# Gate matrix of an expert layer: indirect stores in place of one-hot products

## The reference

```
def peer_ffn(h, w_query, sub_keys, u_tab, v_tab):
    q = (h @ w_query).reshape(bsz, seq, 8, 2, 128)
    scores = einsum('blhcd,hckd->blhck', q, sub_keys)          # 8 heads, 2 halves, 128 keys
    s_top, i_top = top_k(scores, 16)
    cand_s = s_top[..., 0, :, None] + s_top[..., 1, None, :]   # 16 x 16 pairs
    cand_i = i_top[..., 0, :, None] * 128 + i_top[..., 1, None, :]
    best_s, pos = top_k(cand_s, 16)
    expert_idx = take_along_axis(cand_i, pos)
    gates = softmax(best_s)
    act = gelu(einsum('td,thkd->thk', h, u_tab[expert_idx]))
    return einsum('thk,thkd->td', gates * act, v_tab[expert_idx])
```

## Time and profile before

| what | value |
|---|---|
| median of 3 executions | 4148.32 us (4144.81 to 4148.98) |
| the profiled execution | 4145.28 us |
| its span, first to last instruction | 4143.5 us |
| stage one of the expert layer | about 2592 to 3417 us |
| stage two | 3419 us to the end |
| mean granted clock of TensorE | 0.946 of full speed |

### The profile page before, as it was taken

One profiled execution on the slowest core, in us unless ns is written; L12 is line 12 of the kernel. 1 busy time (PEld: TensorE's weight loads), 2 busy tenths in 40 slices (PEclk: granted clock), 3 DMA queues, 4 the chain that ended last, 5 costly groups with the idle time before them and its releaser, 6 DMA issues. The chain is left out here.

```text
span 4143.5 us, 48110 instructions
## 1 busy us (share of the span) xinstructions
PE 3751.7 (91%) x17280; PEld 3022.6 (73%) x17280; DVE 2600.6 (63%) x3745; ACT 1820.0 (44%) x1842; POOL 114.1 (3%) x171
## 2 busy tenths in 40 slices
PE   8779529999999999992999769999999999999999
PEld 4567427777777777771988547888888887888887
DVE  7326539999999999994442542887877534444444
ACT  1226217777777777771332422244444432222222
POOL 0000020000000000002000000000000000000000
PEclk9899759999999999995999779999999999999999
DMA  7410139999999999986322012344444446556554
GB/s 300 146 52 1 47 131 338 362 358 361 363 359 359 360 360 358 362 332 230 102 92 82 1 66 92 135 160 163 172 162 183 160 180 211 188 181 199 185 182 142
DMA packets 222108, 851.13 MB, mean 205 GB/s; under 512 B 19536, under 2 KB 89424, under 8 KB 146832
## 3 DMA queue, kind: packets, MB, share of 16 engines
q1 hardware_dynamic: 202800, 756.94, 51.1%
q10 hardware_dynamic: 9216, 58.72, 3.4%
q0 software_dynamic: 9952, 33.57, 2.4%
HBM read 745.91 MB, written 103.25 MB: 205 GB/s over the span
## 5 line engine op out<-in xcount | busy, mean ns | idle before, releaser
L1384 DVE TENSOR_TENSOR w_low<-w_raw,w_high 128x2048 fp32r<-128x2048 f32 x399 | 909.3, 2290 | 142.4 <-ACT w_high L1313 137.8
L1313 ACT ACTIVATE w_high<-w_raw 128x2048 fp32r<-128x2048 f32 x399 | 764.5, 1916 | 337.2 <-PE ps L125 190.3
L2335 DVE TENSOR_TENSOR uv_lo<-uv_raw,uv_hi 128x2048 fp32r<-128x2048 f32 x128 | 293.3, 2292 | 655.2 <-ACT uv_hi L2192 655.0
L123 PE MATMUL ps<-w_high,xT_high 128*128 128x512 f32 x1056 | 433.7, 411 | 21.1 <-issue 21.1
L124 PE MATMUL ps<-w_low,xT_high 128*128 128x512 f32 x1056 | 418.4, 396 | 0.0
L125 PE MATMUL ps<-w_high,xT_low 128*128 128x512 f32 x1056 | 417.9, 396 | 0.0
L123 PE MATMUL ps<-h4T_high,uv_hi 128*128 128x512 f32 x1024 | 410.4, 401 | 0.5 <-DVE uv_lo L2335 0.5
L123 PE MATMUL ps<-uv_hi,w_hi 128*128 128x512 f32 x1024 | 405.1, 396 | 2.6 <-issue 2.6
L125 PE MATMUL ps<-uv_hi,w_lo 128*128 128x512 f32 x1024 | 405.0, 396 | 0.0
L124 PE MATMUL ps<-uv_lo,w_hi 128*128 128x512 f32 x1024 | 405.0, 395 | 0.0
L125 PE MATMUL ps<-h4T_high,uv_lo 128*128 128x512 f32 x1024 | 399.4, 390 | 0.0
(11 more groups left out here) (481 smaller groups left out, 6281.7 us busy)
## 6 DMA issues: line engine op xcount, KB each, us to landing
w_raw<-in_w_gate_up SPq DMA_DIRECT2D x267, 1024.0 KB, 7.0
w_raw<-in_w_down SPq DMA_DIRECT2D x132, 1024.0 KB, 6.8
uv_raw<-in_peer_u SPq DMA_DIRECT2D x64, 1024.0 KB, 5.1
uv_raw<-in_peer_v SPq DMA_DIRECT2D x64, 1024.0 KB, 4.9
a_rows<-a_out SPq DMA_DIRECT2D x128, 256.0 KB, 2.1
g_rows<-spread ACTq DMA_DIRECT2D x16, 2048.0 KB, 6.5
qT<-g_rows SPq DMA_DIRECT2D x32, 1024.0 KB, 8.9
qT<-a_rows SPq DMA_DIRECT2D x64, 512.0 KB, 8.2
```

Source lines behind the costliest of these rows:

```text
L123: pe.matmul(out, l_hi, r_hi, start=first, stop=False)
L1313: act.activation(w_hi[:, n % SPLIT, :], w_raw[:, n % RAW, :], ACT.Copy).then_inc(s_wh, 1)
L1384: dve.tensor_tensor(w_lo[:, n % SPLIT, :], w_raw[:, n % RAW, :], w_hi[:, n % SPLIT, :].bitcast(F32), ALU.subtract).then_inc(s_wl, 1)
L2335: dve.tensor_tensor(uv_lo[:, n % 2, :], uv_raw[:, n % 2, :], uv_hi[:, n % 2, :].bitcast(F32), ALU.subtract).then_inc(s_lo, 1)
```

## The change

One-hots, gate products, their spreading and the turned selections are removed. In their place:

- A region of 32 MB in DRAM (`gates`) is filled with zeros by 32 stores of 1 MB on SP's queue, beside the first attention. GpSimd clears the source, 128 x 2048, ahead of it. SP waits for the zeros in the next block.
- VectorE works out for each picked expert of a token its place in that region. For each of the 8 heads it compares its 16 experts with all 128 of the token, adds up the gates of those that are equal and in the same or a later head, and sends a value whose expert already stood in an earlier head to a spare place behind the region.
- GpSimd stores the sums with indirect DMAs, 16 for each head, tile by tile: 4 x 8 x 16 = 512, each of 128 values of 4 bytes.
- A plan by estimated costs places VectorE's 45 steps of each tile, 8.2 us to a group.
- The first load of gates waits for all 512 stores, and reads whole rows of the new layout.

```diff
+    gates_flat = nc.dram_tensor("gates", [P * P * SEQ + SEQ * SEL, 1], F32, kind="Internal").ap()
+    gates = gates_flat[0:P * P * SEQ, :].rearrange("(p x) o -> p (x o)", p=P)
...
+    zeros = sb(stage, "zeros", [P, 4 * SEQ])
+    s_z0, s_gz = sem("zeros_here"), sem("gates_zeroed")
...
+            pool.memset(zeros[:, :], 0.0).then_inc(s_z0, 1)
...
+            sp.wait_ge(s_z0, 1)
+            for n in range(P // 4):
+                sp.dma_start(gates[:, n * 4 * SEQ:(n + 1) * 4 * SEQ], zeros[:, :]).then_inc(s_gz, 16)
...
+            sp.wait_ge(s_gz, 16 * (P // 4))
...
+    FIRST, SECOND, BEST, BEST_PLACES, BEST_SECOND, PASS = 4.0, 2.6, 3.4, 3.9, 3.7, 2.3
+    COSTS = [FIRST, SECOND] * 4 + [BEST, BEST_PLACES, BEST_SECOND] * 2 + [1.5 * PASS, PASS, PASS] * 2 + [1.0 * PASS]
+    COSTS += [x for h in range(PH) for x in (PASS, PASS + 0.9, PASS * (PH - h) / PH)]
+    UNIT_EXP, A_STEP = 14, 8.2
+    plan, scores_at, exp_at, spent, turn_of = [[] for _ in range(NG)], {}, {}, 0.0, [(i, x) for i in range(TT) for x in range(len(COSTS))]
+    for i, x in turn_of:
+        n = int(spent // A_STEP)
+        assert n < NG - 1
+        plan[n].append(i)
+        if x == 0 and i:
+            scores_at[n - 1] = i
+        if x == UNIT_EXP:
+            exp_at[n] = i
+        spent += COSTS[x]
...
             def load_weights(p):
                 if p == 0:
                     sp.wait_ge(s_scr, 4 * TT)
-                    sp.wait_ge(s_gst, 16 * (SEQ // HALF))
-                else:
-                    if p >= 2:
-                        sp.wait_ge(s_wf, 2 * (p - 1))
+                    for i in range(TT):
+                        sp.wait_ge(s_put[i], 16 * SEL)
+                elif p >= 2:
+                    sp.wait_ge(s_wf, 2 * (p - 1))
                 for m in (2 * p, 2 * p + 1):
                     sp.wait_ge(s_ast[m % NA], 16 * (m // NA + 1))
                 if p % 2 == 0:
                     q = p // 2
-                    sp.dma_start(g_in[:, q % 2, :].rearrange("p (h x) -> p h x", h=SEQ // HALF),
-                                 g_rows.rearrange("h p x -> p h x")[:, :, 2 * p * HALF:(2 * p + 4) * HALF])\
-                      .then_inc(s_gin[q % 2], 16)
+                    sp.dma_start(g_in[:, q % 2, :], gates[:, 2 * p * SEQ:(2 * p + 4) * SEQ]).then_inc(s_gin[q % 2], 16)
                 sp.dma_start(a_in[:, p % 2, :, :], a_rows.rearrange("m p n -> p m n")[:, 2 * p:2 * p + 2, :])\
                   .then_inc(s_ain[p % 2], 16)
 
...
+        @block.gpsimd
+        def _(pool):
+            pool.iota(token_f[:, :], [[P, TT]], base=0, channel_multiplier=1, allow_small_or_imprecise_dtypes=True).then_inc(s_tok, 1)
+            pool.iota(aside_f[:, :, :], [[P * SEL, TT], [1, SEL]], base=P * P * SEQ, channel_multiplier=SEL,
+                      allow_small_or_imprecise_dtypes=True).then_inc(s_tok, 1)
+            for i in range(TT):
+                for h in range(PH):
+                    pool.wait_ge(s_tot, i * PH + h + 1)
+                    for k in range(PT16):
+                        x = h * PT16 + k
+                        pool.indirect_dma_start(gates_flat, bass.IndirectOffsetOnAxis(ap=place[:, i % 2, x:x + 1], axis=0),
+                                                total[:, i % 2, h, k:k + 1], None).then_inc(s_put[i], 16)
...
-            def gate_products(r):
-                s = r % HOTS
-                pe.wait_ge(s_hot, 5 * (r + 1))
-                if r >= 2:
-                    pe.wait_ge(s_gt2, r - 1)
-                for q in range(4):
-                    mm = pe.matmul(ps[:, 6 + r % 2, q * P:(q + 1) * P], first_hot[:, s, q, :], second_hot[:, s, q, :],
-                                   start=True, stop=True)
-                mm.then_inc(s_gb, 1)
...
-                        if k % 2 and j * 4 + k // 2 in places[n]:
-                            gate_products(rounds.pop(0))
-                    if j == 0 and n in sel_at:
-                        turn_selected(sel_at[n])
...
-            def spread_round(r):
-                act.wait_ge(s_gb, r + 1)
-                h, at = divmod(r, RN)
-                if h and at == 0:
-                    act.wait_ge(s_gst, 16 * h)
-                act.activation(spread[:, :, 4 * at:4 * at + 4].rearrange("p k n -> p n k"),
-                               ps[:, 6 + r % 2, :].rearrange("p (n k) -> p n k", n=4), ACT.Copy).then_inc(s_gt2, 1)
-                if at == RN - 1:
-                    act.wait_ge(s_gt2, r + 1)
-                    act.dma_start(g_rows[h, :, :], spread_flat).then_inc(s_gst, 16)
...
+                first_k, second_k, gate_of = (sel[:, c, :, :].rearrange("p h k -> p (h k)") for c in range(3))
+                st(dve.scalar_tensor_tensor(out=second_k, in0=first_k, scalar=float(PK), in1=second_k, op0=ALU.mult, op1=ALU.add))
+                if i == 0:
+                    dve.wait_ge(s_tok, 2)
+                st(dve.scalar_tensor_tensor(out=place_f[:, :], in0=second_k, scalar=float(SEQ),
+                                            in1=token_f[:, i:i + 1].to_broadcast([P, SEL]), op0=ALU.mult, op1=ALU.add))
+                st(dve.tensor_tensor(to_aside[:, :], aside_f[:, i, :], place_f[:, :], ALU.subtract))
+                if i >= 2:
+                    dve.wait_ge(s_put[i - 2], 16 * SEL)
                 yield
-                yield
-
-            def one_hots(r):
-                s, i = r % HOTS, r * 4 // P
-                if r * 4 % P == 0:
-                    dve.wait_ge(s_selh, i + 1)
-                if r >= HOTS:
-                    dve.wait_ge(s_gb, r - HOTS + 1)
-                for q in range(4):
-                    token = 4 * r + q
-                    dve.tensor_scalar(first_hot[:, s, q, :], iota_row[:, :], selT[:, 0, token:token + 1],
-                                      selT[:, 2, token:token + 1], ALU.is_equal, ALU.mult).then_inc(s_hot, 1)
-                dve.tensor_tensor(second_hot[:, s, :, :], iota_row[:, :].unsqueeze(1).to_broadcast([P, 4, P]),
-                                  selT[:, 1, 4 * r:4 * r + 4].unsqueeze(2).to_broadcast([P, 4, P]), ALU.is_equal)\
-                   .then_inc(s_hot, 1)
+                for h in range(PH):
+                    own = slice(h * PT16, (h + 1) * PT16)
+                    st(dve.tensor_tensor(same, sel[:, 1, h, :].unsqueeze(2).to_broadcast([P, PT16, SEL]),
+                                         second_k.unsqueeze(1).to_broadcast([P, PT16, SEL]), ALU.is_equal))
+                    yield
+                    if h:
+                        st(dve.tensor_reduce(seen[:, :], same[:, :, 0:h * PT16], AX.X, ALU.add))
+                        st(dve.scalar_tensor_tensor(out=seen[:, :], in0=seen[:, :], scalar=0.0, in1=to_aside[:, own], op0=ALU.is_gt,
+                                                    op1=ALU.mult))
+                        st(dve.tensor_tensor(place_f[:, own], place_f[:, own], seen[:, :], ALU.add))
+                    st(dve.tensor_copy(place[:, i % 2, own], place_f[:, own]))
+                    rest_of = same[:, :, h * PT16:SEL]
+                    st(dve.tensor_tensor(rest_of, rest_of, gate_of[:, h * PT16:SEL].unsqueeze(1).to_broadcast([P, PT16, SEL - h * PT16]),
+                                         ALU.mult))
+                    yield
+                    st(dve.tensor_reduce(total[:, i % 2, h, :], rest_of, AX.X, ALU.add))
+                    dve.sem_inc(s_tot, 1)
+                    yield
...
-                gates = g_in[:, q % 2, :].rearrange("p (h j n) -> p h j n", h=SEQ // HALF, j=2 * GROUP)
+                gates_in = g_in[:, q % 2, :].rearrange("p (j n) -> p j n", j=2 * GROUP)
                 for j in range(GROUP):
                     if p:
                         dve.wait_ge(s_wl, 2 * (p - 1) + j + 1)
-                    dve.tensor_tensor(wf[:, j, :].rearrange("p (h n) -> p h n", n=HALF),
-                                      a_in[:, p % 2, j, :].rearrange("p (h n) -> p h n", n=HALF), gates[:, :, p % 2 * GROUP + j, :],
-                                      ALU.mult).then_inc(s_wf, 1)
+                    dve.tensor_tensor(wf[:, j, :], a_in[:, p % 2, j, :], gates_in[:, p % 2 * GROUP + j, :], ALU.mult).then_inc(s_wf, 1)
...
-                    for kind, i, c in plan[n]:
-                        for x in range(c):
-                            if kind == "T":
-                                next(tiles[i])
-                            else:
-                                one_hots(i + x)
+                    for i in plan[n]:
+                        next(tiles[i])
```

More of the change, by code:

```diff
@@ L923, in emit, with _ @@
     with nc.Block() as block:
+        @block.sync
+        def _(sp):
+            sp.wait_ge(s_z0, 1)
+            for n in range(P // 4):
+                sp.dma_start(gates[:, n * 4 * SEQ:(n + 1) * 4 * SEQ], zeros[:, :]).then_inc(s_gz, 16)
         attend(block, "heads_mixed", 16, 2, lambda i: HD if i < 8 else 2 * HD, HD, head_cols,
@@ L2143, in _ @@
                 pe.wait_ge(s_lo, n + 1)
-                rounds = list(rounds_in[n])
```

(1 more changed line is left out.)

84 lines of the change are left out of this document (15 added, 69 removed).

## The result

The changed kernel takes **4372.85 us** (median of four, 4364.43 to 4401.17) against 4148.65 (4144.81 to 4149.15): ratio 1.0558, 95% interval 1.0536 to 1.0579. Slower was right, and the time lies inside the wide range (4190 to 4380), though not inside the forecast's own (4210 to 4343); the forecast was +108 us and +224 came, so half of the loss has a cause that the sum doesn't hold. The profiled execution took 4375.07 us, its span is 4373.3.

What follows compares the result with a forecast made beforehand. TensorE, gapless in the activation stage, was taken to bound the kernel; afterwards GpSimd's 512 stores would. 4145.3 + 107.6 (later output stage) + 1.3 (lower clock) = 4254.2, about 4256 us; own range 4210 to 4343, wide range 4190 to 4380.

Steps and rivals of the forecast that it cites:

- TensorE's 118 us: Activation stage of the expert layer: removing 1024 gate products, 128 rounds of four, takes 118 us off TensorE.
- VectorE at 0: Activation groups: VectorE's new list, 8.2 us a group beside a 2.29 us subtraction, fits TensorE's 10.88 us; cost 0.
- zeros at 0: First attention, 310 to 420 us: 32 zero stores of 1 MB take 104 us on SP's idle queue; cost 0.
- Holding of stores by two-input instructions: GpSimd's stores beside VectorE: those begun during a two-SBUF-input instruction wait for its end, 1.72 us a store instead of 1.26.
- rival 1: GpSimd's stores beside VectorE: no holding, stores keep to 1.26 us; 4089 us, faster; chance 0.14.
- Load to first product, 12.3 us: Start of the output stage: from issue of the gates' load to TensorE's first product, taken unchanged at 12.3 us.
- up to 4 us quicker: Gates' load before the output stage: its longer rows could save up to 4 us, left out of the sum.
- if nothing else becomes late, activations end at 3298.6: Activation stage: with gate products gone and no other engine late, it ends at 3298.6 instead of 3416.9 us.
- existing scatter of 16: Kernel before, from 557.61 us: 16 indirect stores of token numbers, used to price a store at 0.96 + 0.30 us.
- rival 2: DMA side during the stores: 4-byte writes queue behind 1 MB loads, 2.1 us a store; 4510 us; chance 0.14.
- GpSimd never runs dry: GpSimd's 512 stores: they follow without waiting for VectorE, from 2690.9 to 3512.7 us.

Runs made afterwards that it cites:

- nap_each: The changed kernel with a short GpSimd clearing (128 x 1 values, 0.12 us) behind every store, no wait for landing: 4250.9 us, ratio 1.0257.
- no_stores: The changed kernel without the 512 indirect stores; GpSimd only counts the semaphores up and the gates stay zero: 4030.99 us, ratio 0.9714.
- psum_break_6: `break_6` with the second inputs of VectorE's long comparisons and products read from PSUM instead of SBUF: 4295.99 us, ratio 1.0354.
- half_scattered: The changed kernel with tiles 0 and 1 by stores, landing wait every 6th, tiles 2 and 3 by one-hots and gate products as before: 4091.62 us, ratio 0.9868.
- break_6: The changed kernel with GpSimd waiting for the landing of its stores behind every 6th store of a tile: 4348.09 us, ratio 1.0479.
- few_16: The changed kernel with all 512 stores, each storing 16 values instead of 128, other gates staying zero: 4187.83 us, ratio 1.0099.

## Why the prediction went as it did, point by point

| step | forecast | changed kernel | `nap_each` (no stretch) |
|---|---|---|---|
| first to last Gelu, us | 701.6 | 954.8 | 701.6 |
| first store | 2690.9 | 2694.1 | 2689.8 |
| us a store, tile 0 | 1.82 | 1.81 | 1.81 |
| tile 1 | 1.70 | 1.31 | 1.70 |
| tile 2 | 1.63 | 1.48 | 1.66 |
| tile 3 | 1.26 | 1.53 | 1.28 |
| last store starts | about 3511.4 | 3637.6 | 3512.7 |
| output stage starts | 3527.1 | 3649.0 | 3524.1 |
| time | 4256 | 4373 | 4251 |

- **TensorE's 118 us, VectorE at 0, zeros at 0**: right (`no_stores`; the stretch 310 to 420).
- **Holding of stores by two-input instructions**: right in mechanism and in size, to 0.03 us a store in each tile. `psum_break_6` shows that it is VectorE's SBUF operands: 180 ns a store gone without an edit to the stores. The rule of the Trainium skill, page "SBUF — State Buffer", section "Who interferes with whom", that a two-SBUF-input instruction contends with GpSimd's reading of SBUF, agrees; the sentence there that a tensor_tensor doesn't stall the making of descriptors (rival 1) doesn't carry over to indirect stores. Rival 1 is out: 1.81 beside VectorE, not 1.26.
- **Load to first product, 12.3 us**: 9.0 in the changed kernel (3639.96 to 3648.96). The "up to 4 us quicker" not taken was there.
- **The step that failed** is "if nothing else becomes late, activations end at 3298.6", with its use in the sum: the four tiles' stores were laid beside a TensorE and a VectorE that the stores can't touch. The existing scatter of 16 was the only row of the form, and 16 stores last 20 us; what 128 a tile do to others it couldn't show. The row was used for GpSimd's time, where it was right, and silently also for the others' time. That the time still lies inside 4190 to 4380 is luck: the upper end was put there for rival 2, a slower store, and no store was slower; in the stretches the stores kept 1.26 us and everybody else stood. Rival 2 came nearer in time alone: that the DMA side can't take this many isn't shown, and the load of 1 MB at 3017.32 came in 4.7 us.
- **Which wait took its place**: GpSimd's for VectorE, 162.3 us ahead of tiles 2 and 3, since VectorE stood with the others. The forecast's "GpSimd never runs dry" fell by this alone.
- **Slips in the working** that change nothing: 118.3 us by 128 rounds are 0.92 us, not 0.91, and rival 1's 3186 + 161.3 is 3347.3.

What the stretches are is settled only in part. Shown: they need indirect DMAs, reading or writing, whatever the addresses; GpSimd's being busy isn't enough; they don't come from TensorE's instruction packets being late by its own count of matmuls; with pauses for landing every 6 or 12 stores none came in four kernels (one of these, `half_scattered`, has none without pauses either); every 24 wasn't enough in one. Not shown: what is clogged, why TensorE and VectorE still start one instruction in 1.4 us, what delayed the Gelu at 2932, and a threshold, since the changed kernel and `nap_each` had the same pace of stores and only one of them was caught. That few values prevent it was seen at 16 and 64 values of a store, but they may have escaped by timing, too.

One rival stands untested: the recording itself. Every execution compared here, the timed ones too, has a span and a clock from the profiler's records, so none ran unrecorded. All nine kernels with stretches have lost many of the landing counts (at most 4308 of 8192 are there); of the others `break_6` (6510) and `psum_break_6` (5720) have lost some and the rest nearly none (99 at most). In the changed kernel the loss begins with the first stores: 1156 of the 2048 counts of tile 0 are there, although TensorE went at full pace. Engines held until their records are out would look like these stretches. Against it speaks `few_16`, whose stores leave as many records each (32 packets and 16 counts) and stopped nobody. A run without the profiler would decide it.

## What to carry to other kernels

A row of the trace prices an operation for its own engine; before 512 of them are laid beside a full TensorE, ask of the longest stretch in which the trace shows them beside others, and keep a rival in which they stop everybody. An indirect DMA in a row costs GpSimd 1.14 us with 16 values and 1.26 with 128, and more beside VectorE instructions with two SBUF inputs, so it is the count of such DMAs that must fit. When two ways of doing a job load different engines and either alone sets the end, split the job: half the tiles by stores and half by TensorE took 4092 us, against 4145 and 4373 for either alone.

## What the runs showed of the hardware that was not expected

- Many indirect DMAs beside other work, in a recorded execution, can bring TensorE, ScalarE and VectorE nearly to a stand: TensorE 8.2 us busy of 40, one matmul in 2.8 us with releaser "issue", clock 0.50, while GpSimd goes on at 1.26 us a store. TensorE and VectorE then start one instruction in 1.4 us each; the one load of 1 MB that was issued between (3017.32) came in 4.7 us. The state outlasts the last store by 9 to 14 us.
- In the changed kernel each stretch went on to the last store of its tile; standing engines don't hold the stores. Executions of one kernel that have it spread by up to 64 us (4329 to 4393; 4364 to 4401), those of a kernel without it by 10 at most (4291.0 and 4301.0).
- A clearing of 0.12 us between two stores is free: it fits into the gap of 0.30 us.
- The store in a row: 0.96 us + 0.30 with 128 values, 0.89 + 0.30 with 64, 0.84 + 0.30 with 16.
